# Order of an expert's weight loads in a two-block transformer kernel: the down matrix moves between gate and up matrix of the next expert

## What is computed

```python
# 32 experts in 4 groups; each token goes to 2 experts of one group
def block_ffn(args):
    tok, e = args
    xb = xt[tok]
    hb = jax.nn.silu(xb @ w1[e]) * (xb @ w3[e])
    return hb @ w2[e]
```

## Time and profile before

| | before |
|---|---|
| median of 3 executions | 2617.99 us (2616.46 to 2620.15) |
| profiled execution | 2615.25 us |
| its span in the trace | 2613.5 us |
| mean granted TensorE clock | 0.975 |
| TensorE busy | 2486.7 us (95%) |
| VectorE busy | 1391.6 us (53%) |
| ScalarE busy | 1155.1 us (44%) |
| all DMA | 414.33 MB, mean 159 GB/s |
| expert matrices and their like (L3097) | 99 loads of 2048 KB |

### The profile page before, as it was taken

One profiled execution on the slowest core, in us unless ns is written; L12 is line 12 of the kernel. 1 busy time (PEld: TensorE's weight loads), 2 busy tenths in 40 slices (PEclk: granted clock), 3 DMA queues, 4 the chain that ended last, 5 costly groups with the idle time before them and its releaser, 6 DMA issues.

```text
span 2613.5 us, 28455 instructions
## 1 busy us (share of the span) xinstructions
PE 2486.7 (95%) x11190; PEld 1939.7 (74%) x11190; DVE 1391.6 (53%) x1971; ACT 1155.1 (44%) x1578; POOL 111.2 (4%) x163
## 2 busy tenths in 40 slices
PE   7999999999998999999999999999999799999993
PEld 6867888888787787888887778877887466666652
DVE  5587443343434754434457464354346577777754
ACT  4387332222435743212233243333244577777752
POOL 0111000000140000000000000000001000000001
PEclk9989999999998999999999999999999899999996
DMA  4300233434331023232222122222304999999983
GB/s 146 129 1 26 88 113 118 140 97 146 129 113 41 2 98 105 73 133 73 93 97 98 63 105 97 104 74 93 125 11 184 395 420 429 429 430 429 428 351 114
DMA packets 147281, 414.33 MB, mean 159 GB/s; under 512 B 10667, under 2 KB 75334, under 8 KB 134342
## 3 DMA queue, kind: packets, MB, share of 16 engines
q1 hardware_dynamic: 141078, 391.17, 39.3%
q0 software_dynamic: 3296, 12.58, 1.3%
q10 hardware_dynamic: 2768, 8.69, 0.9%
HBM read 380.70 MB, written 31.72 MB: 158 GB/s over the span
## 4 chain that ended last, share of the span: by engine, by line
PE 77%; DVE 9%; DMA 7%; ACT 4%; issue 3%; POOL 0%; ACTq 0%; POOLq 0%; DVEq 0%; SPq 0%
PE ps L320 20%; PE ps L321 20%; PE ps L322 20%; PE ps L2795 6%; DMA area<-in_w 6%; DVE area L2691 2%; PE ps L1002 1%; PE ps L1978 1%; PE ps L2733 1%; PE ps L2735 1%; PE ps L1685 1%; PE ps L968 1%; PE ps L1658 1%; PE ps L2127 1%; ACT area L2804 1%
## 5 line engine op out<-in xcount | busy, mean ns | idle before, releaser
L322 PE MATMUL ps<-area,area 128*128 128x512 f32 (+2 forms) x1712 | 660.9, 386 | 0.0
L345 DVE TENSOR_TENSOR area<-area,area 128x2048 fp32r<-128x2048 f32 (+4 forms) x161 | 341.1, 2119 | 553.3 <-ACT area L339 553.3
L339 ACT ACTIVATE area<-area 128x2048 fp32r<-128x2048 f32 (+4 forms) x161 | 284.3, 1766 | 557.0 <-PE ps L322 552.6
L321 PE MATMUL ps<-area,area 128*128 128x512 f32 (+3 forms) x1368 | 527.2, 385 | 0.0
L320 PE MATMUL ps<-actT_parts,area 128*128 128x512 f32 (+1 forms) x984 | 386.5, 393 | 7.7 <-DVE area L345 3.4
L321 PE MATMUL ps<-actT_parts,area 128*128 128x512 f32 (+1 forms) x984 | 383.6, 390 | 0.0
L322 PEld LDWEIGHTS ps<-area,area 128*128 128x128 f32 (+1 forms) x1712 | 321.2, 188 | 66.3
L2691 DVE TENSOR_TENSOR area<-area,area 128x2048 fp32r<-128x2048 f32 x132 | 299.8, 2284 | 34.7 <-ACT area L2686 34.5
L321 PEld LDWEIGHTS ps<-area,area 128*128 128x128 f32 x1368 | 259.2, 190 | 49.5
L320 PE MATMUL ps<-area,area 128*128 128x512 f32 (+2 forms) x728 | 277.8, 382 | 5.2 <-DVE area L743 5.2
L2686 ACT ACTIVATE area<-area 128x2048 fp32r<-128x2048 f32 x132 | 250.9, 1907 | 30.3 <-DMA area<-in_w 29.3
(11 more groups left out here) (344 smaller groups left out, 2680.1 us busy)
## 6 DMA issues: line engine op xcount, KB each, us to landing
area<-in_w SPq DMA_DIRECT2D x99, 2048.0 KB, 13.3
area<-in_w_in SPq DMA_DIRECT2D x16, 2048.0 KB, 7.5
area<-in_l_w_gate SPq DMA_DIRECT2D x22, 1024.0 KB, 5.2
area<-in_l_w_up SPq DMA_DIRECT2D x22, 1024.0 KB, 7.7
area<-in_l_w_in SPq DMA_DIRECT2D x9, 2048.0 KB, 8.2
expert_inputs<-maskz SPq DMA_DIRECT2D x24, 512.0 KB, 8.4
area<-in_l_w_down SPq DMA_DIRECT2D x8, 1536.0 KB, 7.0
area<-in_l_w_down SPq DMA_DIRECT2D x8, 1280.0 KB, 6.2
```

What stands on the lines that cost most here:

```text
L321: pe.matmul(dst(r), a.l, b.h, start=False, stop=False)
L322: m = pe.matmul(dst(r), a.h, b.l, start=False, stop=end)
L339: eng.activation(w.h, raw, ACT.Copy).then_inc(w_hi, 1)
L345: dve.tensor_tensor(w.l, raw, w.high_f, ALU.subtract).then_inc(w_lo, 1)
```

## The change

One line of the list of loads. Before, the three matrices loaded for one step are gate n+1, up n+1, down n; after, they are gate n+1, down n, up n+1. `place_of`, the slots, the semaphores and what each load waits for follow from the list. The number of loads, the order of work on the four compute engines and the explicit calls load(3), load(5), load(4) at the start stay, so load(3) becomes down 0 (was up 1) and load(4) up 1 (was down 0).

```diff
             order = [(0, 0), (0, 1)]
             for n in range(NE):
-                order += [(n + 1, 0), (n + 1, 1), (n, 2)] if n + 1 < NE else [(n, 2)]
+                order += [(n + 1, 0), (n, 2), (n + 1, 1)] if n + 1 < NE else [(n, 2)]
             for n in range(NE, NE + NOVER):
                 order += [(n, j) for j in range(3)]
```

## The result

The changed kernel takes 2719.32 us (median of 4, 2718.15 to 2734.61) against 2617.6 of the kernel before (2616.46 to 2620.15): ratio 1.0401, 95% interval 1.0363 to 1.0438. It is slower by 102 us; 2707.8 was forecast, with a range of 2662 to 2745. The profiled execution took 2718.15 us, its span is 2716.4, against 2615.25 and 2613.5.

A forecast was written before the change was run, and what follows sets the result against it. The matrices' transfer at 430 GB/s was taken to set the pace, TensorE just behind. Start 8.4, loop 64.4 and clock 17 gave +89.8 us on 2615.25; with 2.7 for the median, 2707.8 us, range 2662 to 2745.

The forecast's parts named there:

- The changed wait and the loop: Expert stage: gate n+3 waits for down n, the queue runs dry; 18.35 us per expert, +64.4 us.
- The 29 intervals: Down 0 to down 29: each goes from 16.13 to 18.35 us, +64.4 us, with slow clock added besides.
- The clock's term: TensorE in the expert stage: idle gaps lower its clock, 1.7 us each, taken 10 times, +17 us.
- The start: First experts: up 1 loads in down 0's place, so down 0 starts later, +8.4 us.
- The end: Behind down 29: all is loaded or in flight, so 0 us, with +5 as bound.
- The restart of a dry queue: Gate load issued on an empty SyncE queue: lands after 8.1 us, range 7.8 to 8.5.
- rival (b): Expert loads: a free queue restarts faster, a load lands in 7.1 to 7.6 us; 2662 us, chance 0.12.
- Rival (c): Expert stage: clock lost at every expert, period 20.45 us, +134 us, 2752 us; chance 0.11.
- Rival (a): Expert stage: not slower, the queue swallows the later issue and down 0's wait ends; 2611.6 us, chance 0.05.

The follow-up runs named there:

- copy-first run: Changed kernel, with ScalarE's copy for down n moved ahead of its split of gate n+2: 2714.79 us, ratio 1.0387.
- half-filled kernel: Changed kernel plus unused filler products on TensorE, 3 before an even expert's down product and 2 before the next gate product: 2704.77 us.
- a kernel of its own: Kernel before, with only the first step of the load list changed: 2627.26 us, ratio 1.0036.
- two filled pairs: Changed kernel with 10 or 5 filler products per two experts, each without and with the list's first step restored: 2729.65 and 2718.29 us; 2704.77 and 2695.15 us.
- four-slot chain: Kernel before, with its old load list but four slots in place of five: 2726.95 us, ratio 1.041.
- first-step run: Changed kernel, with only the first step of its load list put back as before: 2720.86 us, ratio 1.0381.

## Why the prediction was right, and where its sizes were off

**The changed wait and the loop: right.** Gate n+3 is issued when down n ends, in bursts of three. The load issued at 2507.76 lands after 8.08 us, forecast 8.1; landing to the end of the down product was 10.22, forecast 10.25. All 29 gate loads that wait for down 0 to down 28 are issued as that product ends; they land after 7.7 to 8.7 us, 8.15 on average, and in 24 of 29 cases the next down product starts 3.0 to 3.2 us after the landing. SyncE waits for down products alone. The rate is 354 GB/s (forecast 372, for intervals of 18.35 and not 19.28 us). That the DMA share is 0.88, as forecast (0.87), is chance: in proportion to the rate it would be 0.83.

**The 29 intervals**: forecast 64.4 for the loop and 17 for the clock, 81.4; measured 91.3. This is the mis-sized term, by 10 us, and 10 of the 11.5 us by which the result lies above the forecast. The changed kernel's rows divide it. The loop's own part has 1.5 us more, for landings of 8.15 in place of 8.1. The clock's term counted ten slow down products at 1.7 us each. Of down 0 to 28 just ten were slow (1, 2, 4, 6, 8, 10, 12, 14, 16, 18), but they took 8.54 to 10.11 us, 19.3 in all above 7.15; that it was ten is luck, for the count was only taken between bounds of 0 and 29. The remaining 6.3 us are a cost that the sum did not have: behind down 20, 22, 24, 26 and 28, which ran at full speed, the next down product starts 4.0 to 5.0 us after the gate's landing. There the slow clock fell on the gate product. Ahead of down 25 the chain has

```profile
2530.66 0.47 PE ps L2733
2531.13 0.41 PE ps L2735
2531.54 0.43 PE ps L2733
2531.97 0.43 PE ps L2735
```

with 0.43 us per matmul where it is otherwise 0.23. ScalarE's copy for down 25, with which the loop's own path ends, is done at 2537.40, 0.9 us before down 25 starts at 2538.31:

```profile
2536.80 0.60 ACT L2784 ACTIVATE area<-ps 128x512 f32<-128x512 f32 x1
```

So this time TensorE's own work set the start. The eight slow matmuls of that gate product took 1.6 us more than fast ones. They started only at 2530.66, behind the token rows, which stand behind the split of the burst's third load (landed at 2525.82); the copy-first run shows that this second link is nearly as long as the first. Together the three parts make 27.1 us over the 64.4, measured 26.9.

The half-filled kernel agrees in size: it took 0.61 us from each interval, 17.7 us in all. It is no clean price of the clock, as the filler adds work of its own and two down products were still slow.

**The start**: forecast 8.4; measured 9.6 in the changed kernel (10.75 less 1.14), 10 as a kernel of its own, and 11.4 and 9.6 in the two filled pairs, which are less clean. The miss of 1.2 is the clock again, which I had left out there. TensorE had stood idle for 15 us, and in the chain the product of up 1 that then follows runs at 0.43 us per matmul for most of its first ten. Down 0 behind it then ran at full speed, 7.03 us and not 9.29 as before, so that by its end the delay is 7.4 us; the forecast had only said that nothing comes on top.

**The end**: forecast 0; 27.06 against 27.05 us.

**The restart of a dry queue**: rival (b) wanted 7.1 to 7.6 us. The 29 gate loads of the changed kernel took 7.7 to 8.7, the one of the four-slot chain 8.31, and up 1 at the start 8.36. The Trainium skill's fixed 2.0 us plus bytes over 436 GB/s ("DMA: Bandwidth & Descriptors", Anatomy of one DMA), which it gives for GpSimd's path, would be 6.8 as an estimate. None of these loads from SyncE's queue landed so soon.

**Rival (c)**, a slow clock in every expert, fell: 0.95 mean clock, ten slow down products of 29, intervals of 19.28 and not 20.45. **Rival (a)**, no slowdown, fell on the number that it was to be decided by: the issue comes 10.2 us after the gate's landing, and 7.8 was the latest that would do.

## What to carry to other kernels

In a ring of slots, fetching something earlier than its user can take it is not free: it shifts a late release onto another load. Write down for each load whose slot it takes and when that one is used up; if release plus one transfer on a free queue is more than the time until the queue runs dry, the whole ring slows down, though no engine is full. And where an engine works off a list by hand, look for a step that makes the slot's last user wait for a later load: two edits of ScalarE's list gave back 39 of 102 us.

## What was not expected of the hardware

The clock's drops are irregular. That they make these kernels noisier isn't shown: the executions of the first-step run spread by 13 us and those of the changed kernel by 16, but the kernel before spreads by 17 over 17 executions and the one with four slots, where slow down products are most frequent, by 6. The length of the gap alone doesn't tell where the drop falls: a gap of 3.21 us was followed by a down product at full speed (2518.93, 7.13 us) with the slow matmuls in the gate product behind it, gaps of 3.29 and 3.41 by products of 8.83 and 9.81 us. Extra work of no use, 5 filler products per two experts, made the kernel 15 us faster: the clock was 0.99 and not 0.95, and two of the 29 down products were slow and not ten.
